# Softmax normalisation on ScalarE, and a last product taken by token halves, in a one-core transformer layer

## What is computed

```python
sh_m, sc_m, gt_m, sh_f, sc_f, gt_f = split(silu(c) @ mod_w + mod_b, 6)
h = rms_norm(x, g0) * (1 + sc_m) + sh_m
q, k, v = h @ w_qkv                      # 32 query heads, 8 key heads of 64, rotary
p = softmax([q k^T / 8 (own chunk of 64 and the one before), sink])[..., :-1]
x = x + gt_m * rms_norm((p @ v) @ w_o, g1)
h = rms_norm(x, g2) * (1 + sc_f) + sh_f
gate, up = split(h @ w_in, 2)            # hidden width 5632
x = x + gt_f * rms_norm((silu(gate) * up) @ w_out, g3)
```

## Time and profile before

| | us |
|---|---|
| median of 3 runs (lowest, highest) | 1140.44 (1139.5, 1140.71) |
| the profiled execution, its own time | 1141.52 |
| its span in the trace | 1139.7 |
| busy: TensorE, VectorE, ScalarE, GpSimd | 1066.1, 697.2, 467.5, 63.0 |

### The profile page before, as it was taken

How to read it: one execution, slowest core, us unless ns; L and a number is a source line. 1 busy time by engine, 2 the same in 40 slices (tenths; PEclk the granted TensorE clock), 3 DMA queues, 4 the chain that set the end, 5 groups by cost and what they waited for, 6 DMA issues and landing times.

```text
span 1139.7 us, 13583 instructions
## 1 busy us (share of the span) xinstructions
PE 1066.1 (94%) x4968; PEld 844.9 (74%) x4968; DVE 697.2 (61%) x866; ACT 467.5 (41%) x554; POOL 63.0 (6%) x59
## 2 busy tenths in 40 slices
PE   5788899898897799999999999999999999999995
PEld 2555766576685588888888888888888888888884
DVE  2686777978897836676675444445443555445544
ACT  4322454443553643443333333333334433444333
POOL 0000012301210100000000000000001000000002
PEclk9899999998999999999999999999999999999998
DMA  9999999997797327787776555555555455555532
GB/s 363 416 416 416 416 362 388 404 353 263 286 356 295 130 92 259 268 314 264 295 304 212 187 184 199 189 188 194 184 185 185 167 202 184 186 196 205 185 147 74
DMA packets 50599, 288.23 MB, mean 253 GB/s; under 512 B 6401, under 2 KB 6401, under 8 KB 23937
## 3 DMA queue, kind: packets, MB, share of 16 engines
q1 hardware_dynamic: 47090, 268.47, 63.4%
q0 software_dynamic: 2304, 16.78, 3.6%
q10 hardware_dynamic: 1168, 2.49, 0.6%
HBM read 285.36 MB, written 2.10 MB: 252 GB/s over the span
## 4 chain that ended last, share of the span: by engine, by line
PE 77%; DVE 8%; DMA 8%; ACT 3%; issue 2%; POOL 1%; SPq 0%; DVEq 0%; ACTq 0%; POOLq 0%
PE ps L1271 24%; PE ps L1272 24%; PE ps L1273 24%; DMA mraw<-in_mod_w 4%; DMA graw<-in_mod_h 4%; PE ps L1294 3%; DVE wlo L718 3%; DVE mraw L729 2%; ACT whi L399 2%; PE ps L1328 1%; PE ps L1428 1%; PE ps L1304 1%; DVE nT L769 0%; PE ps L1317 0%; DVE wlo_in L718 0%
## 5 line engine op out<-in xcount | busy, mean ns | idle before, releaser
L718 DVE TENSOR_TENSOR wlo<-raw,whi 128x1024 fp32r<-128x1024 f32 x336 | 400.5, 1233 | 308.7 <-ACT whi L399 308.7
L1271 PE MATMUL ps<-whi,hThi 128*128 128x512 f32 x1232 | 488.5, 396 | 20.4 <-DVE wlo L718 18.0
L399 ACT ACTIVATE whi<-raw 128x2048 fp32r<-128x2048 f32 x168 | 321.5, 1916 | 413.3 <-PE ps L1273 390.8
L1273 PE MATMUL ps<-whi,hTlo 128*128 128x512 f32 x1232 | 483.0, 392 | 0.0
L1272 PE MATMUL ps<-wlo,hThi 128*128 128x512 f32 x1232 | 482.9, 392 | 0.0
L1271 PEld LDWEIGHTS ps<-whi,hThi 128*128 128x128 f32 x1232 | 233.4, 189 | 85.9 <-issue 35.1
L1273 PEld LDWEIGHTS ps<-whi,hTlo 128*128 128x128 f32 x1232 | 233.1, 189 | 49.6
L1272 PEld LDWEIGHTS ps<-wlo,hThi 128*128 128x128 f32 x1232 | 233.7, 190 | 47.3
L729 DVE CUSTOM_DVE_ANT_0 mraw<-mraw,cb,mbias 128x1024 f32<-128x1024 f32 x64 | 88.0, 1389 | 45.0 <-DMA mraw<-in_mod_w 45.0
L729 DVE CUSTOM_DVE_ANT_0 mraw<-mraw,cb,modT 128x1024 f32<-128x1024 f32 x64 | 83.6, 1318 | 20.6 <-DMA mraw<-in_mod_w 20.4
L1271 PE MATMUL ps<-whi,oThi 128*128 128x512 f32 x112 | 46.6, 416 | 9.2 <-DVE wlo L718 9.2
(11 more groups left out here) (150 smaller groups left out, 535.1 us busy)
## 6 DMA issues: line engine op xcount, KB each, us to landing
raw<-in_w_in SPq DMA_DIRECT2D x88, 1024.0 KB, 4.8
mraw<-in_mod_w SPq DMA_DIRECT2D x128, 512.0 KB, 7.6
raw<-in_w_out SPq DMA_DIRECT2D x44, 1024.0 KB, 4.8
raw<-in_w_qkv SPq DMA_DIRECT2D x24, 1024.0 KB, 11.4
graw<-in_mod_h SPq DMA_DIRECT2D x16, 1024.0 KB, 14.7
graw<-in_mod_h POOLq DMA_DIRECT2D x16, 1024.0 KB, 8.7
raw<-in_w_o SPq DMA_DIRECT2D x16, 1024.0 KB, 7.2
x<-in_x ACTq DMA_DIRECT2D x2, 1024.0 KB, 8.9
```

Source lines behind the costliest of these rows:

```text
L399: A(split_of(q, s)[0], raw[:, s], ACT.Copy).then_inc(hi_done, 1)
L718: V.tensor_tensor(low[:, k], raw[:, s, k], high[:, k].bitcast(F32), ALU.subtract).then_inc(done, 1)
L1271: mm(dst, hi, high[:, n], start=start, stop=False)
L1273: return mm(dst, lo, high[:, n], start=False, stop=stop)
```

## The change

`normalise` moves from GpSimd's program to ScalarE's. There it is eight instructions for each (i, x), one for each tile of `pS`, each a copy with `den` as its scale; GpSimd's loads of gate rows now follow one another. The last iteration of `f2` takes blocks 0 and 1 as before, waits for blocks 2 and 3, and then takes both for token half 0 and both for half 1. At the end VectorE multiplies each bank by the gate row as soon as ScalarE has squared it (`gated_y2`), and when the inverse root is there one instruction scales and adds (`out_y2`). One of the eight pieces, (1, 3), is scaled by ScalarE and added by GpSimd. All of half 0 is now VectorE's. SyncE stores (1, 3) ahead of (1, 2).

```diff
# sync: stores
-            for b in range(HB):
-                for e in range(NB):
-                    if e < POOL_ADDS[b]:
-                        sp.wait_ge(y2_pool, POOL_ADDS[0] * b + e + 1)
-                    else:
-                        sp.wait_ge(y2_step, 5 * b + NB + e - POOL_ADDS[b] + 1)
+            for b, e, done, count in ((0, 0, y2_step, 1), (0, 1, y2_step, 2), (0, 2, y2_step, 3), (0, 3, y2_step, 4),
+                                      (1, 0, y2_step, 5), (1, 1, y2_step, 6), (1, 3, y2_pool, 1), (1, 2, y2_step, 7)):
+                sp.wait_ge(done, count)
# scalar
+            def normalise(i, x):
+                act.wait_ge(r_ready, 2 * i + x + 1)
+                for u in range(2):
+                    for t in range(4):
+                        s = pS[:, x, u, t, 0:keys_of(x, t)]
+                        p = A(s, s, ACT.Copy, scale=den[:, x, u, t:t + 1])
+                    p.then_inc(p_act, 1)
...
+                if i:
+                    normalise(i - 1, 0)
+                    normalise(i - 1, 1)
                 hi_of(g + 2)
...
+            normalise(2, 0)
+            normalise(2, 1)
             hi_of(26)
             pT_out(2)
...
             hi_of(29)
+            normalise(3, 0)
+            normalise(3, 1)
             hi_of(30)
...
+            act.wait_ge(y2rs, 2)
+            act.wait_ge(y2_gated, 8)
+            A(gated(1, 3), gated(1, 3), ACT.Copy, scale=rstd[:, 5:6]).then_inc(y2_scaled, 1)
# vector
+            def gated_y2(b, *es):
+                for e in es:
+                    dve.wait_ge(y2sq, NB * b + e + 1)
+                    V.tensor_tensor(gated(b, e), ps[:, NB * b + e], grow[:, e * N:(e + 1) * N],
+                                    ALU.mult).then_inc(y2_gated, 1)
...
-                    V.scalar_tensor_tensor(gated(b, e), ps[:, NB * b + e], rstd[:, 4 + b:5 + b],
-                                           grow[:, e * N:(e + 1) * N], ALU.mult, ALU.mult).then_inc(y2_step, 1)
-                for e in range(POOL_ADDS[b], NB):
...
-                    V.tensor_tensor(x1[:, b, cs], x1[:, b, cs], gated(b, e), ALU.add).then_inc(y2_step, 1)
+            def out_y2(b, e):
...
+                V.scalar_tensor_tensor(x1[:, b, cs], gated(b, e), rstd[:, 4 + b:5 + b], x1[:, b, cs], ALU.mult,
+                                       ALU.add).then_inc(y2_step, 1)
+            gated_y2(0, 0, 1, 2, 3)
+            mean_y2(0)
+            for e in range(NB):
+                out_y2(0, e)
+            gated_y2(1, 0, 1, 2)
+            mean_y2(1)
+            gated_y2(1, 3)
+            out_y2(1, 0)
+            out_y2(1, 1)
+            out_y2(1, 2)
# gpsimd
-            def normalise(i, x):
-                pool.wait_ge(r_ready, 2 * i + x + 1)
-                for u in range(2):
-                    G.tensor_tensor(pS[:, x, u], pS[:, x, u], den[:, x, u].unsqueeze(2).broadcast_to([P, 4, P]),
-                                    ALU.mult).then_inc(p_act, 1)
...
+            pool.wait_ge(y2ms, 2)
+            inv_root(rstd[:, 5:6], stat[:, 11:12], y2rs)
+            pool.wait_ge(y2_scaled, 1)
+            G.tensor_tensor(x1[:, 1, 3 * N:], x1[:, 1, 3 * N:], gated(1, 3), ALU.add).then_inc(y2_pool, 1)
# tensor, f2
-                for s in range(4):
+                for s in range(2 if end else 4):
...
+                if end:
+                    for s in (2, 3):
+                        hidden_ready(s)
+                    for b in range(HB):
+                        for s in (2, 3):
+                            part(s, b)
```

More of the change, by code:

```diff
@@ L191, in build @@
         gk_hi, gk_lo = sem("gk_hi"), sem("gk_lo")
-        y2_bank, y2sq, y2sum, y2ms, y2rs, y2_step, y2_pool, stored = (
-            sem(n) for n in ("y2_bank", "y2sq", "y2sum", "y2ms", "y2rs", "y2_step", "y2_pool", "stored"))
+        y2_bank, y2sq, y2sum, y2ms, y2rs, y2_step, y2_pool, y2_gated, y2_scaled, stored = (
+            sem(n) for n in ("y2_bank", "y2sq", "y2sum", "y2ms", "y2rs", "y2_step", "y2_pool", "y2_gated", "y2_scaled", "stored"))
         def vector_of(k):
@@ L1132, in _, with mean_y2 @@
             f2(FT // 4 - 1, end=True)
-            for b in range(HB):
+            def gated_y2(b, *es):
[3 more added lines that the diff above has]
+                                    ALU.mult).then_inc(y2_gated, 1)
+            def mean_y2(b):
                 dve.wait_ge(y2sq, NB * (b + 1))
@@ L1139, in _ @@
                                 ALU.add).then_inc(y2ms, 1)
+            def out_y2(b, e):
+                cs = slice(e * N, (e + 1) * N)
                 dve.wait_ge(y2rs, b + 1)
-                for e in range(NB):
-                    V.scalar_tensor_tensor(gated(b, e), ps[:, NB * b + e], rstd[:, 4 + b:5 + b],
-                                           grow[:, e * N:(e + 1) * N], ALU.mult, ALU.mult).then_inc(y2_step, 1)
-                for e in range(POOL_ADDS[b], NB):
-                    cs = slice(e * N, (e + 1) * N)
-                    dve.wait_ge(y2_step, 5 * b + e + 1)
-                    V.tensor_tensor(x1[:, b, cs], x1[:, b, cs], gated(b, e), ALU.add).then_inc(y2_step, 1)
+                dve.wait_ge(y2_gated, GATED_ORDER.index((b, e)) + 1)
+                V.scalar_tensor_tensor(x1[:, b, cs], gated(b, e), rstd[:, 4 + b:5 + b], x1[:, b, cs], ALU.mult,
[10 more added lines that the diff above has]
+            out_y2(1, 2)
         @block.gpsimd
@@ L1194, in _ @@
             load_gate(21)
-            normalise(0, 0)
             load_gate(22)
             load_gate(23)
-            normalise(0, 1)
             load_gate(24)
@@ L1202, in _ @@
             load_gate(27)
-            normalise(1, 0)
             load_gate(28)
             load_gate(29)
-            normalise(1, 1)
             load_gate(30)
             load_gate(31)
[L1209 to L1212, removed]
             pool.wait_ge(vc, 1)
@@ L1247, in _ @@
             diagonals(diag3, 1)
[L1248 to L1254, removed]
+            pool.wait_ge(y2ms, 1)
+            inv_root(rstd[:, 4:5], stat[:, 10:11], y2rs)
+            pool.wait_ge(y2ms, 2)
+            inv_root(rstd[:, 5:6], stat[:, 11:12], y2rs)
+            pool.wait_ge(y2_scaled, 1)
+            G.tensor_tensor(x1[:, 1, 3 * N:], x1[:, 1, 3 * N:], gated(1, 3), ALU.add).then_inc(y2_pool, 1)
         @block.tensor
@@ L1630, in f2 @@
                         last = part(s, b)
-                    if not (end and s == 3):
-                        last.then_inc(pe_done, 1)
+                    last.then_inc(pe_done, 1)
+                if end:
[4 more added lines that the diff above has]
+                            part(s, b)
             f2(0, True, False)
@@ L1643 @@
 WO_ORDER += [(2, 1), (2, 2), (2, 3), (3, 0), (3, 1), (3, 2), (3, 3)]
-POOL_ADDS = (3, 2)
+GATED_ORDER = [(0, 0), (0, 1), (0, 2), (0, 3), (1, 0), (1, 1), (1, 2), (1, 3)]
 X_BANKS = (0, 1, 2, 3, 4, 5, 0, 1)
```

4 lines of the change are left out of this document (2 added, 2 removed).

## The result

| | before | changed kernel |
|---|---|---|
| median of 11 runs each on one chip (lowest, highest), us | 1140.07 (1137.54, 1145.0) | 1132.17 (1129.81, 1137.25) |
| ratio, 95% interval | | 0.9936 [0.9919, 0.9952] |
| span of the profiled execution, us | 1139.7 | 1131.7 |

What follows compares the result with a forecast made beforehand. TensorE bounds it, busy 1066.1 of 1139.7 us, so gains come only where it idles: attention and the end. 1.6 + 2.4 + 2.2 + 2.8 = 9.0 us off gives 1131.4 against the median, range 1128.9 to 1138.0.

Steps and rivals of the forecast that it cites:

- Term 1: Attention before block 25: without GpSimd's normalisation beside it, VectorE is held less, one pair of eight counting; 1.6 us.
- Term 2: TensorE behind the wait for block 25: the shorter wait keeps the clock up for 12 matmuls; 2.4 us.
- rival A: TensorE near 263 us: the clock falls all the same and the clock gain is gone; 1133.8 us, chance 0.14.
- Term 3: Attention's fourth group: ScalarE normalises sooner than GpSimd, so `outputs(3)` begins at 307.0 instead of 309.25; 2.2 us.
- I take nothing off: From 311 to 400 us: attention's 6.2 us gain lasts, as the load queue moves as a whole; 0 us lost.
- rival B: Load queue up to the 12.85 us transfer: attention's gain is all given back; 1137.6 us, chance 0.19.
- Term 4: Kernel's end: new order and gate products finish the additions at 1133.5 instead of 1136.30, despite a 0.8 us stall; 2.8 us.
- rival D: Attention: ScalarE's tiles, at 0.48 us or more, become the bound; slower, 1149.0 us at 1.0 us a tile; chance 0.06.
- C: Whole kernel: attention's gain is given back and the end gains under 2 us, nothing measurable; 1139 us, chance 0.09.

Runs made afterwards that it cites:

- b_lock: Changed kernel, with GpSimd also making products of the same shape at the old places on a tile nobody reads; ratio 0.9946 to the kernel before.
- b_group2: Kernel before, with group 2 alone normalised by ScalarE; ratio 0.9974.
- a_end: Kernel before with only the last iteration's new order and the new end, GpSimd still normalising; ratio 0.9980, 2.3 us faster.
- a_order: Kernel before with only the new order of blocks in the last iteration; ratio 0.9985.
- b_group3: Kernel before, with group 3 alone normalised by ScalarE; ratio 0.9982.
- a_gating: Kernel before with only the new gate products and folded additions at the end, old order of blocks; ratio 1.0001.
- a_attention: Kernel before with only the normalisation moved to ScalarE, last iteration and end unchanged; ratio 0.9954, 5.2 us faster.
- d_same: The changed kernel run once more, unaltered; ratio 0.9931 to the kernel before, median 1134.79 us.
- c_vector_adds: Changed kernel with piece (1, 3) scaled and added by VectorE too, without ScalarE and GpSimd; ratio 0.9893 to the kernel before, from two runs only.
- c_fill: Changed kernel with two banks of block 2 for half 1 put before block 3 for half 0; ratio 0.9914 to the kernel before, two runs only.
- c_wlo_first: Changed kernel with VectorE's rotary step of group 3 put behind `wlo` of block 25 and the reciprocal of (2, 1); ratio 0.9914 to the kernel before.
- c_both: Changed kernel joining c_wlo_first and c_vector_adds; ratio 0.9900 to the kernel before, median 1130.87 us.

## Why the prediction was right

**Term 1, 1.6 us for GpSimd holding VectorE.** 9.99 to 8.36 is 1.63; 1.11 of it is the shorter wait, and 0.52 lies inside block 24, whose `wlo` pair was held. That it is the holding, and not the result that comes sooner, b_lock shows. How it is held can be read in the kernel before: GpSimd's products end at 255.89 and 257.87, and VectorE's two instructions that began beside them end at 256.97 and 258.95, each 1.08 us later. Counting one pair of eight was right for block 25, and b_group2 shows it apart.

**Term 2, 2.4 us for the clock, failed in its reason.** "I expect the clock to stay up", said the prediction, with a wait of 1.2 us. The wait was 1.73 us, for the reason just given, and the clock fell all the same in the profiled execution: rival A, in part, since it came back within the half block. The step from the length of one wait to the clock does not hold at all, as the runs show. After 2.84 us it fell for the whole half block (before, 10.94), for a part of it (a_end, a_order, b_group3 and b_lock, 9.92 to 9.94) or not at all (a_gating). That last in the stretch of 263 to 266 us:

```profile
263.00:266.00 3.00, 2.75 (x12) 2.28 (x13) 2.96 (x8) 0.00 (x0) 1.36 (x1) 1.00 0.27 71
```

After 1.73 us it fell in two kernels (changed, b_group2) and stayed in four (a_attention, d_same, c_vector_adds, c_fill, 8.37 each). The size was well put for when it stays: terms 1 and 2 together are 9.99 + 10.94 - 8.36 - 8.37 = 4.20, forecast 4.0. In the profiled execution term 2 is 1.02. Part of it is not the clock's: a_gating at full clock has 9.72, because `p_turn(2)` then waits 1.1 us for GpSimd's products, so a full clock alone would have brought the kernel before 1.2 us.

**Term 3, 2.2 us for group 3, was mis-sized: 2.87.** The place and the order of events were as told. The term took a tile at 0.34 us; eight follow one another in 2.45 us, so (2.45 - 0.39) / 7 = 0.29 us apart, where 0.39 is the length of one. The nearest row was that of another function and its accumulator read. But the tiles explain only about half of the 0.67 us. The prediction let all 16 follow one another up to 302.9. In the trace the first eight are over at 297.13, and the others begin only with the reciprocal of (3, 1) at 297.43 and end at 299.88. With the 2.65 us by which `outputs(2)` came earlier added (276.06 to 273.41), that is 302.53, 0.4 us sooner than counted. The remaining 0.3 us lie behind the tiles: `hi` of block 30 and `pT_out(3)` take 3.78 us up to `outputs(3)`, where 4.1 were counted. The Trainium skill ("VectorE: DVE Perf Modes", the section on the TRN2 errata) gives 350 cycles for a ScalarE copy of 128 elements, an estimate of 0.29 us each at the page's 1.2 GHz. The distance in this trace agrees with it. The 0.8 us that the prediction worked out from it, for 16 tiles in a row, did not come, as the reciprocal of (3, 1) stands between the two eights.

**What is given back.** "I take nothing off", said the prediction for the way to 400 us. In the profiled pair 1.44 us are given back (88.83 to 90.27), most of it with the landing of the `mraw` transfer: it comes 38.69 us after `outputs(3)` before and 39.62 after the change, and the rest is what follows it. But the landing lies anywhere from 38.07 to 40.24 among the 14 traces (38.07 to 39.46 in the four kernels where GpSimd normalises, 39.03 to 40.24 in the five with the changed kernel's attention, 39.21 and 38.19 in c_wlo_first and c_both), and a stretch "to norm" follows it by 50.1 to 50.7 us in all but one. Whether the change itself lengthens it is therefore open, between 0 and about 1.4 us; that rival B does not hold is plain, for 4.6 of the 5.5 us gained by then (347.87 to 343.28, with block 24 at 255.13 in both) are still there. From the norm to the last square the changed kernel has 0.18 us less, though TensorE's stall of 0.95 us is in it: the later clock behind the norm cost the kernel before 1.13 us in its profiled execution, which is chance and not the change.

**Term 4, 2.8 us for the end: 2.63.** The last square to the last end went from 9.00 to 5.42, forecast 9.0 to 5.5. From the first matmul of the last iteration to the last square it is 21.96 us before and 22.91 with the change, so the stall costs 0.95 us, forecast 0.8; c_fill has 21.99. Two errors inside the term cancel, which is luck. GpSimd's addition holds one scale-and-add for 1.0 us, not 0.5 (three in 3.08 us, where four alone take 2.74):

```profile
1126.71 1.75 DVE L1171 SCALAR_TENSOR_TENSOR x<-guT,rstd,x 128x512 f32<-128x512 f32 x1
```

It ends 0.55 us after GpSimd's addition of 1126.21 to 1127.91. The Trainium skill ("SBUF — State Buffer", section on two separate sides) says that the shared port is locked for a whole instruction, and that the other engine is blocked meanwhile; this row agrees with it. Against that, the first scale-and-add of half 1 began 2.3 us after the last square's begin, where 2.8 were counted, as the gate products and the mean followed sooner.

**ScalarE as the bound (rival D) and no change (C)** are out: a tile takes 0.29 us where D needed 0.48, and the `hi` of blocks 26 and 30 hold nobody up.

**Sum.** 1.63 + 1.02 + 2.87 + 3.58 + 0.18 = 9.28 us, less 1.44, gives 7.84 of the 8.0 us; the other 0.2 us lie behind VectorE's last end (3.40 us to the end of the span before, 3.20 now). The forecast was 9.0. Terms 1, 3 and 4 make 7.1 us where 6.6 were forecast, so their mechanisms carry the prediction. Term 2 brought 1.0 of 2.4 us in this pair, and 1.44 us that no term had were given back; the 1.13 us of the clock behind the norm made up for part of that by chance. The forecast time came within 0.8 us of the median, which is less than its runs scatter, so a hit as close as that is luck too.

## What to carry to other kernels

Before giving GpSimd an elementwise product "beside" a busy VectorE, look in VectorE's timeline for the same instruction with and without it: if it is longer beside GpSimd, ScalarE with a scale column may be the better place, even in 64 small instructions. At the end of a kernel, ask whose queue is still working on the first half when the second is complete; ordering the matmuls so that the first half is through early was worth twice the shorter arithmetic here, its stall already taken off (2.65 - 0.95 against 0.85). And when runs scatter by more than the effect, measure from one fixed point of TensorE's program to the next instead of the whole time, and compare the granted clock of each stretch before its length is put down to the change.

## What was not expected of the hardware

- TensorE's clock is not a function of the wait just before it: after the same wait of 2.84 us its stretch was 9.72, 9.93 or 10.94 us, and after 1.73 us 8.37 or 9.92. It was at its full level in both kernels without a wait there. Behind the norm before the feed-forward part it is the same: after waits of 4.55 to 4.61 us the clock came back late in three executions (before, a_gating, d_same) and early in four (a_attention, a_order, c_wlo_first, c_vector_adds).
- GpSimd's help can cost more than it takes over. A scale-and-add that takes VectorE 0.68 us by itself was left to GpSimd, whose addition made one of VectorE's instructions 1.0 us longer.
- The start of block 24 moves by 7.7 us between the traces of kernels that are equal up to group 2 or differ only in groups 0 and 1 (252.2 to 259.9), and 4.3 us between two executions of the very same kernel (255.13 and 259.41), while the short stretches behind it, the clock apart, repeat within 0.05 us.
